# Twelve small loads move to ScalarE's queue, two row loads go first, the first norm runs tile by tile, and two matmul groups change places

## What is computed

```python
hn  = rms(x, norm_attn_g)
mix = mixers(hn @ w_in)              # gated DeltaNet (4 heads) and mLSTM (4 heads), with states
x   = x + mix @ w_out
x   = x + moe(rms(x, norm_moe_g))    # top 4 of 32 experts; per expert 12 MB of weights
x   = x + sigmoid(rms(x, norm_ple_g) @ ple_gate_w) * (p @ ple_w)
y   = rms(x, final_norm_g)
```

## Time and profile before

| | us |
|---|---|
| median of 3 runs | 1337.69 |
| lowest, highest | 1335.25, 1337.87 |
| profiled execution, whole time | 1334.51 |
| profiled execution, span | 1332.8 |
| PE busy | 1280.2 (96%) |
| DVE busy | 530.3 (40%) |
| ACT busy | 206.4 (15%) |
| POOL busy | 46.3 (3%) |

### The profile page before, as it was taken

How to read it: one execution, slowest core, us unless ns; L and a number is a source line. 1 busy time by engine, 2 the same in 40 slices (tenths; PEclk the granted TensorE clock), 3 DMA queues, 4 the chain that set the end, 5 groups by cost and what they waited for, 6 DMA issues and landing times.

```text
span 1332.8 us, 17039 instructions
## 1 busy us (share of the span) xinstructions
PE 1280.2 (96%) x6270; PEld 545.5 (41%) x6270; DVE 530.3 (40%) x1160; ACT 206.4 (15%) x410; POOL 46.3 (3%) x102
## 2 busy tenths in 40 slices
PE   6999998889899999999999999999999999999997
PEld 4764787634333333333333333333333333333333
DVE  2682446654733333343323233332323433333233
ACT  2451101042110111110011110001101100111112
POOL 5100002000000000000000000000000000000000
PEclk9999999888999999999999999999999999999999
DMA  8421111046699999999999999999999999999941
GB/s 255 136 85 63 63 64 63 13 168 252 215 429 427 429 428 428 428 429 428 428 429 428 428 429 429 428 430 427 429 428 429 428 428 429 428 429 428 429 166 40
DMA packets 56517, 438.30 MB, mean 329 GB/s; under 512 B 12586, under 2 KB 19895, under 8 KB 31882
## 3 DMA queue, kind: packets, MB, share of 16 engines
q1 hardware_dynamic: 56490, 437.93, 79.3%
HBM read 432.89 MB, written 5.02 MB: 329 GB/s over the span
## 4 chain that ended last, share of the span: by engine, by line
PE 62%; DMA 31%; DVE 4%; issue 2%; ACT 1%; SPq 1%; POOL 0%; DVEq 0%; POOLq 0%; ACTq 0%
DMA ring<-in_expert_w_gu 30%; PE bank L1110 21%; PE bank L1121 8%; PE bank L594 8%; PE bank L1096 3%; PE bank L1066 3%; PE bank L592 2%; PE bank L770 1%; PE bank L1131 1%; PE bank L1219 1%; PE bank L679 1%; PE bank L691 1%; PE bank L1074 1%; PE bank L689 1%; PE bank L1099 1%
## 5 line engine op out<-in xcount | busy, mean ns | idle before, releaser
L1110 PE MATMUL bank<-ring,SC 128*64 128x512 f32 x2048 | 476.0, 599 | 6.8 <-DVE SC L2048 1.9
L1110 PEld LDWEIGHTS bank<-ring,SC 128*64 128x64 f32 x2048 | 136.3, 136 | 295.0 <-issue 248.6
L1121 PE MATMUL bank<-ring,SC 128*64 128x512 f32 x1024 | 226.8, 595 | 0.0
L2078 DVE TENSOR_TENSOR SC<-bank,bgu 128x256 f32<-128x256 f32 x128 | 48.2, 418 | 224.9 <-PE bank L1131 224.9
L1121 PEld LDWEIGHTS bank<-ring,SC 128*64 128x64 f32 x1024 | 70.6, 137 | 133.3 <-issue 123.3
L594 PE MATMUL bank<-xT,ring 128*128 128x320 f32 x384 | 111.6, 437 | 4.7 <-ACTq L1310 3.7
L2048 DVE TENSOR_TENSOR SC<-bank,gmoe 128x512 f32<-128x512 f32 x33 | 22.8, 692 | 218.1 <-PE bank L1074 218.1
L2065 DVE TENSOR_TENSOR X<-X,bank 128x512 f32<-128x512 f32 x120 | 76.9, 682 | 51.4 <-PE bank L1096 51.4
L1066 PE MATMUL bank<-XS,SC 128*64 128x512 f32 x396 | 92.3, 602 | 2.6 <-DVE SC L2042 2.6
L1427 ACT ACTIVATE SC<-bank 128x512 f32<-128x512 f32 x33 | 19.7, 597 | 462.7 <-PE bank L1066 462.7
L2069 DVE TENSOR_TENSOR X<-X,bank 64x256 f32<-64x256 f32 x120 | 50.2, 418 | 94.9 <-PE bank L1099 93.2
(11 more groups left out here) (482 smaller groups left out, 1030.1 us busy)
## 6 DMA issues: line engine op xcount, KB each, us to landing
ring<-in_expert_w_gu SPq DMA_DIRECT2D x128, 2048.0 KB, 23.5
ring<-in_expert_w_down SPq DMA_DIRECT2D x64, 2048.0 KB, 23.8
ring<-in_w_in SPq DMA_DIRECT2D x7, 2048.0 KB, 7.8
ring<-in_w_out SPq DMA_DIRECT2D x2, 2048.0 KB, 8.5
ring<-in_ple_gate_w SPq DMA_DIRECT2D x4, 1024.0 KB, 14.8
out_gdn_s<-ring SPq DMA_DIRECT2D x1, 2048.0 KB, 9.4
X<-in_x_prompt SPq DMA_DIRECT2D x2, 512.0 KB, 3.8
SC<-in_ple_w SPq DMA_DIRECT2D x1, 1024.0 KB, 5.1
```

The costliest lines, as they stand in the source:

```text
L1110: last = mm(PB[j][SL * h:SL * h + SL, :], xg[:, c % 4, c // 4, :], w[:, FF * h + 512 * j:FF * h + 512 * j + 512], start=(c == 0), stop=(c ...
L1121: last = mm(PB[4][SL * h:SL * h + SL, :], act_t[:, 2 * (c - NGU) + kk, :], w[:, D * kk + 512 * h:D * kk + 512 * h + 512], start=(c == NGU ...
L2078: ins = V.tensor_tensor(out[:, 4 * i:4 * i + 4, :], PB[2 + i][:, :].rearrange("p (k h s) -> p k h s", k=4, h=2)[:, :, h, :], bgu[:, c0 + 4 ...
```

## The change

1. The twelve small loads leave SP's list and are issued at the head of ACT's list.
2. The two row loads are the first on SP's list, ahead of the tokens; PE transposes these rows before `prow`.
3. ACT does a one-column Square of `ones` before it waits for the tokens, so that its table is loaded there.
4. The first norm is done tile by tile: three mean squares, three powers, three scalings, with new semaphores `ms0` and `rs0`. Later counts on `ms` and `rs` go down by one.
5. `ple_part_sample()` stands before `gather(0)` on PE.

```diff
         def _(sp):
+            sp.dma_start(srow[0:24, 0:1536], a["state_conv"].rearrange("o b w c -> (o b w) c")).then_inc(sem("rows_in"), 16)
+            sp.dma_start(srow[32:64, 0:2048], a["expert_b_gu"].rearrange("o e n -> (o e) n")).then_inc(sem("rows_in"), 16)
             for t in range(3):
                 sp.dma_start(X[0:ROWS[t], t, :], tok_dram(x_in, t)).then_inc(sem("x_in"), 16)
...
@@ gpsimd
-            rsqrt("ms", 1, "rs", nst[:, 2, :], nst[:, 1, :])
+            for t in range(3):
+                rsqrt("ms0", t + 1, "rs0", nst[0:ROWS[t], 2, t:t + 1], nst[0:ROWS[t], 1, t:t + 1])
@@ scalar
+            for name, r, n_rows in rows:
+                act.dma_start(prow[r:r + n_rows, :], src).then_inc(sem("params_in"), 16)
+            for i, name in enumerate(["gdn_a_log", "gdn_dt_bias", "mlstm_i_bias", "mlstm_f_bias"]):
+                act.dma_start(bc16[:, 4 * i:4 * i + 4], a[name].to_broadcast([P, 4])).then_inc(sem("small_in"), 16)
+            act.dma_start(w16[:, :, 0:8], w_in[:, :, C_AB:C_AB + 8]).then_inc(sem("small_in"), 16)
+            act.dma_start(w16[:, :, 8:16], w_in[:, :, C_IF:C_IF + 8]).then_inc(sem("small_in"), 16)
             act.wait_ge(sem("consts"), CONSTS["consts1"])
+            link(A(XS[:, 0, 0:1], ones[:, 0:1], ACT.Square))
             act.wait_ge(sem("x_in"), 48)
@@ vector, norm()
-                dve.wait_ge(sem("ss"), 3)
-                tell(V.tensor_scalar(nst[:, 1, :], nst[:, 0, :], 1.0 / D, EPS, ALU.mult, ALU.add), "ms")
-                dve.wait_ge(sem("rs"), 1)
                 for t in range(3):
                     R = ROWS[t]
+                    dve.wait_ge(sem("ss"), t + 1)
+                    tell(V.tensor_scalar(nst[0:R, 1, t:t + 1], nst[0:R, 0, t:t + 1], 1.0 / D, EPS, ALU.mult, ALU.add), "ms0")
+                    dve.wait_ge(sem("rs0"), t + 1)
                     tell(V.tensor_scalar(XS[0:R, t, :], X[0:R, t, :], nst[0:R, 2, t:t + 1], None, ALU.mult), "xs")
```

More of the change, by code:

```diff
@@ L535, in _ @@
             pe.wait_ge(sem("consts"), CONSTS["consts0"])
-            pe.wait_ge(sem("params_in"), 16 * 6)
-            turn(PB[0][:, 0:77], prow[:, :], ident[0:77, 0:77]).then_inc(sem("pcolT"), 1)
             pe.wait_ge(sem("rows_in"), 16 * 2)
@@ L543, in _ @@
             last.then_inc(sem("rows_used"), 1)
+            pe.wait_ge(sem("params_in"), 16 * 6)
+            turn(PB[0][:, 0:77], prow[:, :], ident[0:77, 0:77]).then_inc(sem("pcolT"), 1)
             def turn_x():
@@ L1255, in squares @@
                 return A(scratch[0:R, :], X[0:R, t, :], ACT.Square, accum_out=nst[0:R, 0, t:t + 1])
+            rows = [("norm_attn_g", 0, 8), ("norm_moe_g", 8, 8), ("norm_ple_g", 16, 8), ("conv_w", 24, 48),
+                    ("gdn_norm_g", 72, 1), ("mlstm_norm_g", 73, 4)]
+            for name, r, n_rows in rows:
+                src = a[name].rearrange("o w (c p) -> (o w c) p", p=P) if name == "conv_w" else \
+                    a[name].rearrange("o (c p) -> (o c) p", p=P)
+                act.dma_start(prow[r:r + n_rows, :], src).then_inc(sem("params_in"), 16)
[3 more added lines that the diff above has]
+            act.dma_start(w16[:, :, 8:16], w_in[:, :, C_IF:C_IF + 8]).then_inc(sem("small_in"), 16)
             act.wait_ge(sem("consts"), CONSTS["consts1"])
+            link(A(XS[:, 0, 0:1], ones[:, 0:1], ACT.Square))
             act.wait_ge(sem("x_in"), 48)
```

26 lines of the change are left out of this document (7 added, 19 removed).

## The result

| | before | after |
|---|---|---|
| median | 1337.26 (20 runs, 1330.62 to 1341.63) | 1342.63 (20 runs, 1338.12 to 1346.26) |
| profiled execution, whole time | 1334.51 | 1342.39 |
| profiled execution, span | 1332.8 | 1340.6 |

The ratio after to before is 1.0051, with a 95% interval of 1.0039 to 1.0063. The change costs 0.5%, or 6.8 us by the ratio (the two medians lie 5.4 apart). I had forecast 1335.9, a gain of 1.8, and the result lies outside my range.

What follows compares the result with a forecast made beforehand. The end was taken to be set by when the full stream of expert weights starts, which hangs on SP. Gains 2.8 (first norm) - 1.0 (clock) + 0 (embedding) = 1.8; 1337.69 - 1.8 = 1335.9 us, range 1333.0 to 1338.9.

Steps and rivals of the forecast that it cites:

- the alternation of PE and DVE: Behind the first xT_out in the first norm: stays at 4.5 us, from 17.08 to 21.62 in the kernel before.
- PE reaches L576 at 18.8: End of the first norm: PE comes to the projections at 18.8 us, with 2.8 gained at the start of xT_out.
- third rival: Head, ACT held by its own issues: gain gone at 0.74 us per issue, end 1340.8 at 1.0, 1347 at 1.57; chance 0.12.
- I take a third, 8.4: Tokens' landing before the first norm: between 8.0 and 9.2 us, taken as 8.4 instead of 6.86.
- 8.4 at the latest: ACT's readiness for the first squares: issues end at 5.9, table load and tiny square by 8.4 us, hidden behind the tokens.
- The norm tile by tile: First norm: three rounds of 1.56 us, 4.7 against 3.3 before, with two sums hidden; xT_out starts at 14.2.
- 1.0 lost: PE's first projections partly at half clock after new pauses: between 0 and 2.0 us lost, middle taken as 1.0.
- POOL's last constant: POOL's constants in the head: last at 31.1 instead of 30.22, reader on PE at 33.8, so covered with 2 us left.
- I count 0: Embedding ahead of gather(0): PE may start expert 0 earlier, but 0 us gained at the end; 0 to 2.9 in range.
- The stream of weights: Experts' stage: the end follows SP's issue of expert 1's first pair, 349.26 becoming 347.5, not PE's start on expert 0.
- a mark against me: Sign of failure: first projection moves by 3 and expert 1's first pair doesn't, or the pair moves more than the projections.

Runs made afterwards that it cites:

- e3: The changed kernel with all twelve small loads back on SP behind the tokens, so parts 2 to 5 alone; ratio to the kernel before 0.9991 (0.9970 to 1.0012).
- e1: The changed kernel with only the two w16 loads back on SP, right behind the tokens; ratio to the kernel before 1.0015 (0.9995 to 1.0035).
- e7: Like e3, but on SP the tokens come first, then the row loads, then the twelve small loads; ratio to the kernel before 0.9978 (0.9956 to 0.9999).
- e5: The changed kernel with the two w16 loads at the head of ACT's list instead of its end; ratio to the kernel before 1.0017 (0.9995 to 1.0038).
- e2: The kernel before with only the twelve small loads moved to the head of ACT's list; ratio to the kernel before 1.0024 (1.0002 to 1.0046).
- e11: e7 plus 16 filler transposes in PE's waits between tile halves and ahead of the w16 matmuls; ratio to the kernel before 0.9975 (0.9955 to 0.9995).
- e13: e11 and e12 put together; 1320.96 against 1334.55 for the kernel before, ratio 0.9900 (0.9874 to 0.9926).
- e9: Like e3, but only the state_conv rows ahead of the tokens, the expert_b_gu rows behind them; one time, 1332.24.
- e4: The kernel before with only the sample tile's embedding moved ahead of the first gather; ratio to the kernel before 1.0001 (0.9982 to 1.0020).
- e12: The kernel before with the n_s store and eight m_s stores issued at the end, behind the final gain's load; ratio 0.9952 (0.9927 to 0.9977).
- e6: The changed kernel with SP holding its second weight group until all small_in loads are in; ratio to the kernel before 1.0010 (0.9989 to 1.0030).

## Why the prediction was wrong

**The step that failed first** is the transfers' landing on ACT's queue. My sum let the alternation of PE and DVE stay at 4.5 and went on with "PE reaches L576 at 18.8". That took for granted that `w16` is there: it landed at 27.1, and the 4.54 became 9.48. I priced ACT's issues at length, but for the landing of `w16` I had no term. It stood as one clause of the third rival ("the same comes out if `w16` lands that late"). It was the largest term: +4.94 of +7.19. I had the 3.2 us of landing on SP's queue at hand and took it as a property of the transfer; it is one of the queue and of what runs beside it (4.2 in e3 and 7.2 in e1, still on SP's queue, and 13.8 and 20.2 here).

**"I take a third, 8.4"** for the tokens is the second. The first square came at 12.11. It has three parts. The rows ahead cost 3.4 (e3 against e7), where I put 1.15 from bytes at 356 GB/s. The transfers on ACT's queue beside the tokens add 0.6 in this profile: the tokens landed 8.4 behind an issue at 2.58, at 10.98, in e3 at 10.37. (This part is not firm: in e1 the tokens landed at 12.05, in e5 at 10.6.) ACT, busy with issues to 10.54 and then with its table, adds another 1.13. The range of 8.0 to 9.2 that I gave was built on the assumption that a byte costs the same in any load and leaves the loads behind it as fast as they were.

**ACT's readiness, "8.4 at the latest",** failed with it: 12.07. An issue on ACT cost like one on SP (0.26 to 0.40, the first 0.62) for the first seven, and up to 3.6 us later. My mean of 0.50 was exceeded at (10.54 - 0.77) / 12 = 0.81, beyond the break-even of 0.74 of the rival that ACT is held by its own issues, which I gave 0.12. Its price, 1340.8 to 1347, holds the measured 1342.6, but by luck: the price begins at issues of 1.0 each. At 0.81 its own sum puts the squares at 0.8 + 9.7 + 1.5 = 12.0 and the end at 1337.69 + 0.8 = 1338.5, 1339.5 with the clock. The held ACT accounts for 1.13 of the +3.96 and the late tokens for the other 2.83 (in e2, where the tokens are there at 7.8, the held ACT is the whole of the delay, 11.08 - 8.15 = 2.93); it is the clause on `w16` that carries the time up to what was measured. The row that should have raised it was mine: SP's stall of 12.56 us over eight small broadcasts. I used it as a bound, and then took the other end though no row was nearer to it.

**The norm tile by tile** was sized well. A round is (17.06 - 14.11) / 2 = 1.48, said 1.56; square to `xT_out` 5.62, said 5.8. The 28 row transposes are done at 7.9, said 8. Behind `xT_out` the alternation took 4.75 in e3, said 4.5.

**The clock, "1.0 lost",** was right in kind and too small. In the changed kernel it cost 1.6 (1.09 and 0.51), within my 0 to 2.0; in e2, e3 and e7 it cost 2.8 to 2.9, beyond it. The sentence that the granted clock reads 1.00 in that stretch misreads the view, which has no record there; that the stretch is at the lower level was right. I had reasoned from the moment: a rise by 18.8, or when it rises now. It rose at 20.47 before, when PE had been busy for 6.78 of the 6.90 us from 13.0 to 19.9, and at 30.59 after, behind PE's waits of 1.66 and 5.25. e11 and e13 speak for what PE does ahead of the rise: with the pauses filled it came at 17.85 and 17.16, in e7 at 24.09. But the fillers are not needed for it. e9 has none and rises at 17.26. All this is one profile for each kernel: in before, e4, e9, e11, e12 and e13 the clock rises ahead of the `w16` matmuls and stays up, in after, e1, e2, e3, e5, e6 and e7 behind their start. The Trainium skill, TensorE: Matmul & The Clock Gate, Part 1, says that the point at which the clock rises varies between runs of one kernel. Three kernels here have like heads, before, e4 and e12, and rise at 20.47, 20.52 and 19.34: up to 1.2 us apart. No run here shows two profiles of the same kernel, so e9 may have been luck.

**POOL's last constant** was done at 33.97, said 31.1; its reader stands at 43.8. Covered, with more room than I had said.

**The embedding, "I count 0",** holds: 2.83 us earlier on PE, 0.01 us on the pair, no change in time.

**The stream of weights** holds too: span minus issue of the pair is 983.5 before and between 982.2 and 982.6 in after, e1, e2, e3 and e4. The pair moved by 8.9, the head by 7.2. I had named such a difference as a mark against me. Step by step it is made up so: 7.18 at 243 us, +3.59 up to `out_gdn_s` (308.32 and 319.09), -4.90 up to `out_c_s` (334.59 and 340.46), +2.77 up to `out_n_s` (340.07 and 348.71), +0.27 up to the pair. The +3.59 and the -4.90 come from stretches at half clock, which lie at other places in each execution; the largest of them, of 10.2 us between these two stores, is in before's profile and not in after's. The +2.77 is a gate that I hadn't seen: the pair ahead of `out_n_s` waits until `out_c_s` has landed, and where `out_c_s` follows `out_gdn_s` after 21.4 us it takes 7.8 to 8.1 us to land, otherwise 5.1. The DMA engines are then still full with the pairs issued ahead of it (share 0.99 from 330 to 340 us). So part of what the low clock costs is hidden behind this landing. The time of an execution follows its mean granted clock: the fastest of after, 1338.12, had 0.993, the seven at 0.987 took 1341.95 to 1346.26.

**What stays open.** e3's median is 3.2 us better than its head shift of +2.0 says, and the end of its interval (+1.6) just misses it (in its profile the pair leaves at 349.18, as before, for it lacks the low stretch of 10.2 us); the other kernels with an interval agree with theirs, apart from e12 and e13, whose gain lies elsewhere. Why the tokens are slower behind the row loads was not settled, nor how the last issue on ACT comes to take 3.6 us (in e5, with `w16` first, no issue of ACT takes over 1.28), nor why the DMA engines stay idle behind `out_n_s`, nor what beside the pauses sets the clock at the start.

## What to carry to other kernels

A small load on a second queue isn't free of the large ones on the first: ask when it lands, not only what its issue costs, and put the small loads whose reader is near on the queue and at the place where nothing large runs beside them. Before speeding up the head of a program, find the issue from which the long stream starts; here nine small stores ahead of it were worth 0.48% (0.23 to 0.73), the best head 0.25% (0.05 to 0.45). And where PE alternates with another engine, count its first work at the slow duration, or fill the pauses and look when the clock rises.
